# Four moving operands start 32, 16, 96 and 48 bytes past a multiple of 128 in SBUF, where they started 64 bytes past one

## The chip, the cores and the metric

One core of a Trainium2 chip runs the whole program in one launch. The metric is the device time of that launch in microseconds, taken as the median of several runs. The hardware profile is of one more execution.

## What is computed

Two transformer-like blocks over one sequence of 256 tokens with 1024 features, in float32:

```python
for i in range(2):                       # first block
    h = modulate(rmsnorm(x, norm_mix[i]), sh1, sc1)
    y = pool_mixer(h, ...) if i == 0 else moba_attention(h, w_qkv, w_o, rel_bias)
    x = x + g1 * y
    h = modulate(rmsnorm(x, norm_mlp[i]), sh2, sc2)
    a = relu(h @ w_up[i])                # 1024 -> 4096
    x = x + g2 * ((a * a) @ w_down[i])   # 4096 -> 1024
x = rmsnorm(x, norm_final)
z = rmsnorm(x, norm1) @ w_in + b_in      # second block
...                                      # convolution, linear recurrence (gates wa, wx), two output products
m = sigmoid(z_ga) * y_a + sigmoid(z_gb) * y_b
x = x + m @ w_mix_out
h = rmsnorm(x, norm2)
x = x + (silu(h @ ffn_w1) * (h @ ffn_w3)) @ ffn_w2    # 1024 -> 2816 -> 1024
return rmsnorm(x, norm_f)
```

## The kernel before, in words

**Layout.** Activations lie transposed: 128 features of a chunk on the 128 partitions, 256 tokens along the free dimension. A matmul has a 128x128 block of weights as its stationary operand and one chunk of an activation (128 partitions x 256 columns, 1024 bytes in each partition) as its moving operand. The weights come from HBM as a stream of units of eight such blocks, two units to a DMA, into the ring `raw`.

**Three products instead of one.** Most matrix products are made in a reduced float32 format. Each float32 number is split into a high part and the rest: ScalarE writes `w_hi` from `raw` (line 1104), VectorE writes `w_lo = raw - w_hi` (line 1467), and the activations are split in the same way into pairs such as `hid_hi` and `hid_lo`. A product is then high times high, high times low, low times high:

```python
hi = w[0][:, slot, s * P:(s + 1) * P]
pe.matmul(dst, hi, r_hi, ...)      # line 645
pe.matmul(dst, hi, r_lo, ...)      # line 646
...
lo = w[1][:, slot, s * P:(s + 1) * P]
return pe.matmul(dst, lo, r_hi, ...)   # line 651
```

Each of these matmuls has its own weight load (LDWEIGHTS; the profile calls this engine PEld). In a phase made of whole units the eight chunks' high-weight matmuls come first, 16 of them in turns of lines 645 and 646, and then the eight of line 651: 24 to a unit.

**The split activations.** There are six pairs: `pool` (pool mixer), `xg` (the input of the up projections, qkv, glu, rx, rg, conv and ffn), `hid` (the input of the two down projections), `o` (the input of the attention's output projection), `act` (the input of the gates, and later of the mix product) and `f` (the input of the product with ffn_w2, called w2 here). The number of three-product matmuls they take part in follows from the units: 64 units of 24 for `hid` (1536), 8 for `o` (192), 52 blocks of three for the gates (156) and 8 units for mix (192) for `act`, 22 units for `f` (528), and the work of 174 units for `xg` (4176).

**Where they lie.** `LINE` is 128 bytes and `HALF` is 16 float32 (64 bytes). `w_hi` starts at byte 33,920 of each partition and `w_lo` at 50,304, both multiples of 128; so do all their blocks, 512 bytes apart. Ahead of each split activation a filler of `HALF` elements is allocated at a multiple of `LINE`:

```python
def half_line(name, where=ctx):
    where.enter_context(nc.sbuf_tensor(f"{name}_half_line", [P, HALF], F32, align_bytes=LINE))
```

So `hid_hi` starts at 162,496, `hid_lo` at 195,264, `o_hi` at 189,248, `act_hi` at 119,616 and `f_hi` at 109,248: each 64 bytes past a multiple of 128. Chunks of these are 1024 bytes apart, so every chunk is. The chunks of `xg_hi` and `xg_lo` are 288 float32 (1152 bytes, nine times 128) apart, 64 bytes past a multiple of 128 as well; a matmul of the first block reads 258 columns of them (two more carry the modulation's shift), one of the second block 256. The pool mixer's weights have a place of their own: `pool_w_hi` starts at 196,416 and `pool_hi` at 212,800, so there both the weights and the moving operand are 64 bytes past a multiple of 128, and moving operand and weights differ by a multiple of 128.

**Order of the work.** TensorE goes through the phases pool, up0, down0, qkv with the attention between its units, o, up1, down1, glu, rx, rg, gates, gb, ga, lru, conv, mix, ffn, w2. The products with `raw` itself (last two units of rg, gb, ga and lru; lines 977 and 1030) are full float32 and not split. TensorE waits by semaphores for the split weights (`high_ready`, `low_ready`), for the chunks of the moving operand, and for its output bank to be read. No wait, no queue and no order is touched by the change. The functions that read the four operands are `down` (line 824: `hid`), `o_part` (`o`), the gates' loop and `whole("mix", ...)` (`act`), and `halves` with the loop behind it (`f`). They are written by ScalarE (lines 1207, 1258, 1316, 1420) and VectorE (lines 1662, 1786, 1855, 2052, 2054).

Of the kernel before, what the change touches and what calls it, by code (L numbers as in the profile page):

```python
# [12 lines left out]
F32R = mybir.dt.float32r  # L13

P = 128
SEQ = 256
D = 1024
DC = D // P
FFC = 4 * D // P
RC = 1280 // P  # L20
F2C = 2816 // P
# [8 lines left out]
LINE, HALF = 128, 16  # L30
# [184 lines left out]
def build(nc, weights, w_mod, w_dots, c_row, x_in, vectors, rel_bias, buckets, inv_count, identity, out):  # L215
    scratch = nc.dram_tensor("bias_by_distance", [HEADS, 384], F32, kind="Internal").ap()
    with ExitStack() as ctx:
        def sb(name, shape, dt=F32, where=ctx):
            return where.enter_context(nc.sbuf_tensor(name, shape, dt))
# [5 lines left out]
        def half_line(name, where=ctx):  # L225

            where.enter_context(nc.sbuf_tensor(f"{name}_half_line", [P, HALF], F32, align_bytes=LINE))

        raw = sb("raw", [P, RAW, PAIR])  # L230
        w_hi = ctx.enter_context(nc.sbuf_tensor("w_hi", [P, HL, UT * P], F32R, align_bytes=LINE))
        w_lo = sb("w_lo", [P, HL, UT * P], F32R)
# [47 lines left out]
            pool_hi = sb("pool_hi", [P, DC, SEQ], F32R, part)  # L280
            pool_lo = sb("pool_lo", [P, DC, SEQ], F32R, part)
        with ExitStack() as part:
            half_line("hid", part)
            hid_hi = sb("hid_hi", [P, FFC, SEQ], F32R, part)
            hid_lo = sb("hid_lo", [P, FFC, SEQ], F32R, part)
        with ExitStack() as part:
            qT = sb("qT", [P, 2, SEQ], F32, part)
            kT = sb("kT", [P, 2, SEQ], F32, part)
            vT = sb("vT", [P, 2, SEQ], F32, part)
            vtok = sb("vtok", [P, 2, SEQ], F32, part)  # L290
            toep = sb("toep", [P, 2, 2, 384], F32, part)
            logit = sb("logit", [P, 2, 384], F32, part)
            prob = sb("prob", [P, 2, 384], F32, part)
            probn = sb("probn", [P, 2, 384], F32, part)
            pT = sb("pT", [P, 2, 384], F32, part)
            smx = sb("smx", [P, 2, 8], F32, part)
            half_line("o", part)
            o_hi = sb("o_hi", [P, DC, SEQ], F32R, part)
            o_lo = sb("o_lo", [P, DC, SEQ], F32R, part)
        first.close()  # L300
        with ExitStack() as part:
            RXW = SEQ + RTAPS - 1
            UW = SEQ + TAPS - 1
            rx = sb("rx", [P, RC, RXW], F32, part)
            with ExitStack() as inner:
                half_line("act", inner)
                act_hi = sb("act_hi", [P, RC, SEQ], F32R, inner)
                act_lo = sb("act_lo", [P, RC, SEQ], F32R, inner)
            a2 = sb("a2", [P, RC, SEQ], F32, part)
            sb("behind_a2", [P, RC * SEQ + 2 * HALF], F32, part)  # L310
            u = sb("u", [P, DC, UW], F32, part)
            y = sb("y", [P, DC, SEQ], F32, part)
            grg = sb("grg", [P, RC, SEQ], F32, part)
            rt = sb("rt", [P, RC, SEQ], F32, part)
            ig = sb("ig", [P, RC, SEQ], F32, part)
            av = sb("av", [P, RC, SEQ], F32, part)
            sga = sb("sga", [P, DC, SEQ], F32, part)
            sgb = sb("sgb", [P, DC, SEQ], F32, part)
            pool_prod = sb("pool_prod", [P, 2, POOL_TAPS, SEQ], F32, part)
            h32 = sb("h32", [P, DC, SEQ], F32, part)  # L320
        with ExitStack() as part:
            half_line("f", part)
            f_hi = sb("f_hi", [P, F2C, SEQ], F32R, part)
            f_lo = sb("f_lo", [P, F2C, SEQ], F32R, part)
            yout = sb("yout", [P, DC, SEQ], F32, part)

        four = [ctx.enter_context(nc.psum_tensor(f"bank{b}", [P, 512], F32)) for b in range(4)]
# [1891 lines left out]
```

## Time and profile before

| what | value |
|---|---|
| median of 3 runs | 1018.91 us (1015.68 to 1020.47) |
| span of the profiled execution | 1015.1 us, 20313 instructions |
| TensorE matmul, busy | 978.7 us, 96%, 7980 matmuls |
| TensorE weight load, busy | 934.2 us, 92%, 7980 loads |
| VectorE / ScalarE / GpSimd busy | 77% / 55% / 10% |
| mean granted TensorE clock | 0.985 |

The profiled execution is known by its span, from the first to the last instruction; what lies around it is the 3.8 us up to the median. A matmul's own duration in the profile is a latency, from its start to the modelled end of its output, and matmuls overlap. What a stream of them costs is the distance from start to start.

### The profile page before, as it was taken

Reading aid. Unit: us, or ns where it says so; the run is one execution under the profiler, and the core shown is the slowest. Engines: PE = TensorE matmul, PEld = TensorE weight load, DVE = VectorE, ACT = ScalarE, POOL = GpSimd, SP = SyncE. Lnnn points to the kernel's source line nnn. Section 1 sums busy time; section 2 is a strip of 40 time slices with the busy share of each in tenths; the row PEclk is TensorE's granted clock in tenths of the full one; section 3 lists DMA queues with packets and bytes.
Section 4 is the critical chain, followed back from the end, with each engine's and each line's share of the span. In section 5 each row is a group of like instructions: output and inputs, shape, how many; then the busy total and the mean of one; then the engine's idle time right before and its main releaser. Section 6 shows DMA issues by size and latency. Waiting matters only on the chain.

```text
span 1015.1 us, 20313 instructions
## 1 busy us (share of the span) xinstructions
PE 978.7 (96%) x7980; PEld 934.2 (92%) x7980; DVE 780.2 (77%) x1354; ACT 561.6 (55%) x922; POOL 105.3 (10%) x134
## 2 busy tenths in 40 slices
PE   4799999999999999999999999999999999999996
PEld 1479999999999899999999999998889999999996
DVE  4757986888776777677766799999998887777654
ACT  4248676444666658776454566678116564444352
POOL 0000000000000000000000000899920000000000
PEclk9789999999999999999999999999999999999998
DMA  9997797877465855454545555463445555555631
GB/s 376 421 420 315 268 372 301 343 299 284 126 203 156 306 210 206 167 190 169 212 177 184 174 186 192 141 241 128 139 152 207 184 191 196 179 193 179 208 125 42
DMA packets 35883, 222.31 MB, mean 219 GB/s; under 512 B 3883, under 2 KB 9180, under 8 KB 9436
## 3 DMA queue, kind: packets, MB, share of 16 engines
q1 hardware_dynamic: 35804, 221.22, 60.5%
q8 instruction: 55, 0.90, 0.4%
q14 instruction: 24, 0.20, 0.1%
HBM read 220.13 MB, written 1.07 MB: 218 GB/s over the span
## 4 chain that ended last, share of the span: by engine, by line
PE 82%; DVE 9%; ACT 4%; DMA 3%; issue 2%; DVEq 0%; SPq 0%; ACTq 0%
PE bank L645 23%; PE bank L651 22%; PE bank L646 22%; PE bank L977 5%; PE bank L1030 3%; DVE w_lo L1467 2%; PE s_banks L674 2%; DMA mod_raw<-w_mod 1%; ACT w_hi L1104 1%; DVE s_banks L1872 1%; DVE bank L1847 1%; PE s_banks L1030 1%; DMA raw<-weights 1%; DVE ab L1840 1%; DVE mod_raw L1518 1%
## 5 line engine op out<-in xcount | busy, mean ns | idle before, releaser
L1467 DVE TENSOR_TENSOR w_lo<-raw,w_hi 128x1024 fp32r<-128x1024 f32 x284 | 346.2, 1225 | 31.5 <-ACT w_hi L1104 29.1
L1104 ACT ACTIVATE w_hi<-raw 128x1024 fp32r<-128x1024 f32 x284 | 296.8, 1050 | 102.8 <-PE bank L651 99.9
L645 PE MATMUL bank<-xg_hi,w_hi 128*128 128x258 f32 (+1 forms) x1376 | 341.4, 285 | 1.2 <-DVE w_lo L1467 0.8
L646 PE MATMUL bank<-xg_lo,w_hi 128*128 128x258 f32 (+1 forms) x1376 | 337.0, 282 | 0.0
L645 PEld LDWEIGHTS bank<-xg_hi,w_hi 128*128 128x128 f32 x1376 | 260.2, 189 | 6.2 <-issue 5.1
L646 PEld LDWEIGHTS bank<-xg_lo,w_hi 128*128 128x128 f32 x1376 | 260.6, 189 | 0.2
L651 PE MATMUL bank<-xg_hi,w_lo 128*128 128x258 f32 (+1 forms) x1376 | 198.9, 283 | 0.3 <-DVE w_lo L1467 0.3
L651 PEld LDWEIGHTS bank<-xg_hi,w_lo 128*128 128x128 f32 x1376 | 179.0, 189 | 0.8 <-DVE w_lo L1467 0.5
L645 PE MATMUL bank<-hid_hi,w_hi 128*128 128x256 f32 x512 | 123.5, 279 | 0.0
L646 PE MATMUL bank<-hid_lo,w_hi 128*128 128x256 f32 x512 | 123.4, 279 | 0.0
L646 PEld LDWEIGHTS bank<-hid_lo,w_hi 128*128 128x128 f32 x512 | 96.0, 188 | 0.0
L645 PEld LDWEIGHTS bank<-hid_hi,w_hi 128*128 128x128 f32 x512 | 96.0, 188 | 0.0
L1872 DVE SCALAR_TENSOR_TENSOR s_banks<-u,vec,s_banks 128x256 f32<-128x256 f32 x172 | 71.2, 480 | 0.2
L651 PE MATMUL bank<-hid_hi,w_lo 128*128 128x256 f32 x512 | 70.7, 279 | 0.0
L651 PEld LDWEIGHTS bank<-hid_hi,w_lo 128*128 128x128 f32 x512 | 64.8, 188 | 0.0
L977 PE MATMUL bank<-h,raw 128*128 128x256 f32 x288 | 62.5, 379 | 0.0
L977 PEld LDWEIGHTS bank<-h,raw 128*128 128x128 f32 x288 | 54.6, 190 | 7.3
L605 POOL MEMSET rx<- 128x30 f32 x1 | 0.1, 130 | 560.5 <-PE bank L651 560.5
L624 POOL TENSOR_TENSOR y<-y,pool_prod 128x256 f32<-128x256 f32 x60 | 56.6, 963 | 0.1
L614 POOL TENSOR_TENSOR pool_prod<-u,vec 128x256 f32<-128x256 f32 x60 | 48.0, 822 | 76.2 <-PE bank L651 74.0
L1205 ACT ACTIVATE ub<-ab 128x256 f32<-128x256 f32 x64 | 32.6, 509 | 37.6 <-DVE ab L1655 37.5
L1518 DVE CUSTOM_DVE_ANT_0 mod_raw<-mod_raw,c_all,vec 128x1024 f32<-128x1024 f32 x40 | 49.6, 1276 | 0.0
(246 smaller groups left out, 1301.1 us busy)
## 6 DMA issues: line engine op xcount, KB each, us to landing
raw<-weights SPq DMA_DIRECT2D x157, 1024.0 KB, 5.0
mod_raw<-w_mod SPq DMA_DIRECT2D x28, 1024.0 KB, 11.2
mod_raw<-w_dots SPq DMA_DIRECT2D x20, 1024.0 KB, 8.4
toep<-bias_by_distance SPq DMA_DIRECT2D x8, 256.0 KB, 5.5
x<-x_in SPq DMA_DIRECT2D x1, 1024.0 KB, 5.0
toep<-bias_by_distance SPq DMA_DIRECT2D x8, 128.0 KB, 3.9
y_out<-yout SPq DMA_DIRECT2D x4, 256.0 KB, 2.5
c_all<-c_row SPq DMA_DIRECT2D x1, 512.0 KB, 14.7
```

Source lines behind the costliest of these rows:

```text
L614: nc.gpsimd.tensor_tensor(pool_prod[:, k % 2, e, :], u[:, m, k:k + SEQ], col("dw_w", DC * k + m).broadcast_to((P, SEQ)), ALU.mult).then_in ...
L624: nc.gpsimd.tensor_tensor(dst, dst, pool_prod[:, k % 2, e, :], ALU.add).then_inc(pool_tap, 1)
L645: pe.matmul(dst, hi, r_hi, start=start, stop=False, skip_group_check=True)
L646: pe.matmul(dst, hi, r_lo, start=False, stop=False, skip_group_check=True)
L651: return pe.matmul(dst, lo, r_hi, start=False, stop=stop, skip_group_check=True)
L977: mm = pe.matmul(out_bank(name, v)[:, 0:SEQ], raw[:, slot, ((at % 2) * UT + k) * P:((at % 2) * UT + k + 1) * P], src[:, k, 0:SEQ], start=k ...
L1030: mm = pe.matmul(out_bank("lru", m)[:, 0:SEQ], raw[:, slot, ((at % 2) * UT + s) * P:((at % 2) * UT + s + 1) * P], rt[:, k, :], start=k == ...
L1104: act.activation(pool_w_hi[:, at, :] if name == "pool" and at < 2 else w_hi[:, at % HL, :], raw[:, slot, (at % 2) * UT * P:(at % 2 + 1) * ...
L1205: act.activation(ub[:, j % 2, :], ab[:, j % 2, 0:SEQ], ACT.Relu, bias=ab[:, j % 2, SEQ:SEQ + 1]).then_inc(relu_done, 1)
L1467: ve.tensor_tensor(lo, raw[:, slot, (at % 2) * UT * P:(at % 2 + 1) * UT * P], hi.bitcast(F32), ALU.subtract).then_inc(lo_done, 1)
L1518: ve.tensor_tensor_reduce(w, w, c_all[:], 1.0, col("b_mod", at + half), ALU.mult, ALU.add, accum_out=modv[:, at + half:at + half + 1]).the ...
L1872: ve.scalar_tensor_tensor(dst, u[:, m, k:k + SEQ], col("dw_w", DC * k + m), src, ALU.mult, ALU.add)\
```

## The change

After the change the four pairs `hid`, `o`, `act` and `f` are each one tensor that starts at a multiple of 128 bytes and of which the first `at` float32 are left unused. `at` is 8, 4, 24 and 12, that is 32, 16, 96 and 48 bytes. High and low halves are views of it. The pairs `xg` and `pool` and the weights stay where they are, and the instructions and their order are the same.

```diff
+        def past_line(name, count, at, where):
+            whole = where.enter_context(nc.sbuf_tensor(name, [P, count * SEQ + at], F32R, align_bytes=LINE))
+            return whole[:, at:at + count * SEQ].rearrange("p (c n) -> p c n", n=SEQ)
...
-            half_line("hid", part)
-            hid_hi = sb("hid_hi", [P, FFC, SEQ], F32R, part)
-            hid_lo = sb("hid_lo", [P, FFC, SEQ], F32R, part)
+            hid = past_line("hid", 2 * FFC, 8, part)
+            hid_hi, hid_lo = hid[:, 0:FFC, :], hid[:, FFC:2 * FFC, :]
...
-            half_line("o", part)
-            o_hi = sb("o_hi", [P, DC, SEQ], F32R, part)
-            o_lo = sb("o_lo", [P, DC, SEQ], F32R, part)
+            o = past_line("o", 2 * DC, 4, part)
+            o_hi, o_lo = o[:, 0:DC, :], o[:, DC:2 * DC, :]
...
-                half_line("act", inner)
-                act_hi = sb("act_hi", [P, RC, SEQ], F32R, inner)
-                act_lo = sb("act_lo", [P, RC, SEQ], F32R, inner)
+                act_both = past_line("act_both", 2 * RC, 24, inner)
+                act_hi, act_lo = act_both[:, 0:RC, :], act_both[:, RC:2 * RC, :]
...
-            half_line("f", part)
-            f_hi = sb("f_hi", [P, F2C, SEQ], F32R, part)
-            f_lo = sb("f_lo", [P, F2C, SEQ], F32R, part)
+            f_both = past_line("f_both", 2 * F2C, 12, part)
+            f_hi, f_lo = f_both[:, 0:F2C, :], f_both[:, F2C:2 * F2C, :]
```

The tensors now start at 162,432 (`hid`), 189,184 (`o`), 119,552 (`act_both`) and 109,184 (`f_both`), and the operands that many bytes plus 32, 16, 96 and 48.

## Rows read from the trace of the kernel before

**Rows 1.** The page: busy time, and the granted clock in 40 slices.

```profile
PE 978.7 (96%) x7980; PEld 934.2 (92%) x7980; DVE 780.2 (77%) x1354; ACT 561.6 (55%) x922; POOL 105.3 (10%) x134
...
PEclk9789999999999999999999999999999999999998
```

**Rows 2.** The page: the chain that ended last, by engine.

```profile
PE 82%; DVE 9%; ACT 4%; DMA 3%; issue 2%; DVEq 0%; SPq 0%; ACTq 0%
```

**Rows 3.** Chain of waits, 168 to 264 us, down0: start us, duration us, piece.

```profile
191.85 0.94 PE bank L651 x8
...
205.98 0.94 PE bank L651 x8
208.81 0.94 PE bank L651 x8
...
217.29 0.94 PE bank L651 x8
```

**Rows 4.** Chain of waits, 944 to 1006 us, w2.

```profile
949.69 0.91 PE bank L651 x8
952.41 0.91 PE bank L651 x8
...
966.01 0.91 PE bank L651 x8
```

**Rows 5.** Chain of waits, 797 to 822 us, mix.

```profile
806.01 0.91 PE bank L651 x8
808.74 0.91 PE bank L651 x8
...
819.62 0.91 PE bank L651 x8
```

**Rows 6.** Timeline, 363 to 380 us, o: start us, duration us, engine, line, instruction.

```profile
364.14 0.28 PE L645 MATMUL bank<-o_hi,w_hi 128*128 128x256 f32 x1
...
365.32 0.28 PE L646 MATMUL bank<-o_lo,w_hi 128*128 128x256 f32 x1
...
368.93 0.28 PE L646 MATMUL bank<-o_lo,w_hi 128*128 128x256 f32 x1
...
370.41 0.28 PE L651 MATMUL bank<-o_hi,w_lo 128*128 128x256 f32 x1
```

**Rows 7.** Timeline, 60 to 62 us, pool mixer.

```profile
60.59 0.28 PE L645 MATMUL bank<-pool_hi,pool_w_hi 128*128 128x256 f32 x1
...
61.55 0.28 PE L651 MATMUL bank<-pool_hi,pool_w_lo 128*128 128x256 f32 x1
```

**Rows 8.** Chain of waits, up1 (384 to 472 us), then ffn (850 to 940 us).

```profile
404.68 0.96 PE bank L651 x8
...
439.40 0.96 PE bank L651 x8
```

```profile
865.14 0.94 PE bank L651 x8
...
904.62 0.94 PE bank L651 x8
```

**Rows 9.** Instructions by tile hid_hi, then f_hi: count, duration ns min/median/max, starts.

```profile
L645 PE MATMUL bank<-hid_hi,w_hi x512: 279/279/286, 170.0 to 561.3; 128*128 128x256 f32 x171
L1207 ACT ACTIVATE hid_hi<-ub x64: 417/419/422, 82.2 to 473.3; 128x256 fp32r<-128x256 f32 x48, 128x256 f32 x16
```

```profile
L645 PE MATMUL bank<-f_hi,w_hi x132: 276/276/361, 944.9 to 1003.7; 128*128 128x256 f32 x132
```

**Rows 10.** Timeline, 370.4 to 371.2 us, o, weight loads with matmuls.

```profile
370.52 0.19 PEld L646 LDWEIGHTS bank<-o_lo,w_hi 128*128 128x128 f32 x1
...
370.63 0.28 PE L646 MATMUL bank<-o_lo,w_hi 128*128 128x256 f32 x1
370.64 0.19 PEld L651 LDWEIGHTS bank<-o_hi,w_lo 128*128 128x128 f32 x1
```

**Rows 11.** Timeline, 199.9 to 200.2 us, down0, weight load with its matmul.

```profile
199.93 0.19 PEld L646 LDWEIGHTS bank<-hid_lo,w_hi 128*128 128x128 f32 x1
...
200.05 0.28 PE L646 MATMUL bank<-hid_lo,w_hi 128*128 128x256 f32 x1
```

## The prediction

> **What bounds the kernel now.** The page's busy line and clock line come first: TensorE's matmuls are busy 96% of the span, its weight loads 92%, and the granted clock is at full speed, 2.4 GHz, in all but the first and last slices [rows 1]. The chain that ended last lies on TensorE for 82% of the span [rows 2], and in the stages of this change it runs from matmul to matmul with hardly anything between. So the kernel is as long as its matmuls are apart, and the reader should look at one number, the distance from the start of one matmul to the start of the next. Nothing is removed or added by this change, no wait and no instruction; only where four moving operands begin. It can act only through that distance, and the question is whether the distance depends on the address.
>
> **The distance as it is.** In the chain each unit of 24 matmuls shows once, at its eight matmuls of line 651. In down0 two neighbours start 2.83 us apart, 118 ns to a matmul; over nine units it is 25.44 us / 216 = 117.8 ns [rows 3]. Down1 goes at the same pace. In w2 a unit takes 2.72 us, and six take 16.32 us: 113.3 ns [rows 4]. Mix has 13.61 us for five units: 113.4 ns [rows 5]. The o projection shows both: ten matmuls in 1.18 us, 118 ns, and some 4 us later thirteen in 1.48 us, 114 ns [rows 6]. All these operands lie 64 bytes past a multiple of 128 and their weights on one. So at one alignment there are two steady paces, 117.8 and 113.3 ns, and a stage can stay in the slow one for 1536 matmuls. The durations agree: a matmul with `hid_hi` takes 279 ns, one with `f_hi` 276 [rows 9]. In the fast pace a weight load starts 0.11 us ahead of its matmul and the next load 0.01 us behind that matmul's start [rows 10]; in the slow pace it is 0.12 us [rows 11]. That chain, load, matmul, next load, makes the 113 ns, which is more than the 107 ns that 256 columns take at 2.4 GHz (256 / 2.4). I read 113.3 as the floor of this stream and what lies above it as the two reads getting in each other's way.
>
> **What other addresses cost.** Two stages show it. In the pool mixer, moving operand and weights differ by a multiple of 128 bytes, not by 64 more; at full clock eight matmuls take 0.96 us, 120.0 ns each [rows 7]. And the `xg` operand, whose chunks lie 1152 bytes apart and so change their place against the weights' blocks in every larger power of two, goes at 39.48 us / 336 = 117.5 ns with 256 columns and 34.72 us / 288 = 120.6 ns with 258 [rows 8]. So for 256 columns the trace holds the paces 113.3, 117.5 to 117.8 and 120.0, the last where the difference is 0 modulo 128. None lies at 16, 32, 48 or 96 bytes; their cost has to be bounded between these.
>
> **The change part by part.** Now the terms are: `hid`, 1536 matmuls at 117.8; `o`, 192 at a mixture of the two paces, of which I take 114.5; `act`, 156 in the gates and 192 in mix, 348 together, at 114.2 by the same kind of mixture in the gates; `f`, 528 at 113.4.
>
> I interpolate in a straight line by the distance from 64: 113.3 ns at 64 bytes, 120.0 at 0 (or 128), which is 6.7 ns for 64 bytes, 1.67 ns for each 16. Then:
> - `hid` at 32 bytes, 32 off: 116.7 ns, 1.1 less than now. 1536 x 1.1 = 1.7 us gained.
> - `o` at 16 bytes, 48 off: 118.3, 3.8 more. 192 x 3.8 = 0.7 us lost.
> - `act` at 96 bytes, 32 off: 116.7, 2.5 more. 348 x 2.5 = 0.9 us lost.
> - `f` at 48 bytes, 16 off: 115.0, 1.6 more. 528 x 1.6 = 0.8 us lost.
>
> The sum is +0.7 us, 1018.9 + 0.7 = 1019.6. The profiled execution's span would go from 1015.1 to 1015.8, the 3.8 us around it staying.
>
> The bounds from the same rows. Below: nothing in the trace goes under 113.3, so `hid` can gain at most 4.45 ns, 1536 x 4.45 = 6.8 us, and `o` and `act` 1.2 and 0.9 ns, 0.5 us together: -7.4. Above: all four at the pool mixer's 120.0 is 2.2 x 1536 = 3.4, 5.5 x 192 = 1.1, 5.8 x 348 = 2.0 and 6.6 x 528 = 3.5 us: +10.0. I take the line since the four places lie between the two that are measured, and keep both ends.
>
> The writers of these operands cost nothing: ScalarE's write of `hid_hi` takes 419 ns [rows 9], ScalarE and VectorE are busy 55 and 77% [rows 1], and TensorE hides them. Even 50 ns more on each would meet TensorE only where the first matmul of o waits for its operand. If TensorE got 4% faster in down, the weight splitting (one unit of it per 2.7 us against 1.2 us of VectorE's and 1.0 of ScalarE's time) would still be ahead. Phases whose operands do not move, `xg` above all, have a pattern that repeats from unit to unit, so how they are entered should not matter.
>
> The Trainium skill speaks against all of this. "TensorE: Matmul & The Clock Gate", under the phases of a matmul, says that TensorE reads SBUF through two independent ports and that loading the next weights doesn't steal bandwidth from the running matmul; by that the distance doesn't depend on the two addresses and the sum is 0. The paces in the rows, 113.3 against 120.0, don't agree with it fully, though they don't show that the address is the cause either.
>
> **The rivals.**
> - *The address does nothing.* The paces are then two ways in which the stream falls into step by how a stage is entered, as the o projection shows with both at one alignment [rows 6], and pool's 120.0 comes from its few matmuls behind a halt. Each stage keeps about its pace: 0 us, 1018.9. The port rule of the Trainium skill in the paragraph above is this rival's. Against it: eight times exactly 120.0, a pace seen with 256 columns in no other stage.
> - *`hid` comes loose from the slow pace.* If 32 bytes has no stable slow pace, or one close to 113.3, the down projections gain their 6.8 us, with the others anywhere between -0.5 and +1: 1011.5 to 1013. For it: o and mix leave the slow pace by themselves, and only `hid` stays. Against it: 64 was the one place of which the trace shows the fast pace at all.
 It costs 5.1 us as soon as the four average 118.1 ns (the average now is 2604 matmuls at 116.2, and 5.1 / 2604 is 2.0 ns more), and 10.0 us at 120.0: 1024 to 1028.9. For it: 258 columns, which reach just past a 64-byte piece, cost 3 ns more where two columns at 2.4 GHz are 0.8 [rows 8], and all four new places cross such pieces.
>
> The page "SBUF — State Buffer" of the Trainium skill, under the SBUF cachelines, gives lines of 16 bytes. All four places are multiples of 16, so by that no matmul would touch a line more than now, and this rival's argument from 64-byte pieces falls; no row here shows lines of either size by itself.
>
> **How the numbers follow.** A change within 0.5%, 5.1 us, is about what a measurement of this kernel can't tell from none. The interpolated case, with its own range of 1015.5 to 1023.5 (some stages fast, some slow), gets 0.32; no effect 0.12; `hid` loose 0.24; the collision 0.32. So faster 0.24, same 0.44, slower 0.32. The range takes in both bounds, 1018.9 - 7.4 and 1018.9 + 10.0, trimmed little since both ends are plain cases of their own: 1011.5 to 1028.
>
> **What would show each step.** Right: a unit of the down projections takes about 2.80 us in the chain where it took 2.83, one of w2 2.76 for 2.72, one of mix 2.80, and ffn and up1 stay at 2.82 and 2.89. Wrong: 2.72 in the down projections is the second rival, 2.83 and 2.72 unchanged everywhere is the first, 2.88 in all is the third. A pace below 2.72 us a unit in any stage would show that the floor I took is none. A stage that changes between two paces within itself would say that entering decides more than the address. A change in ffn or up1 of more than 0.02 us a unit would mean that something else than the four operands' places is at work.

## The result, and the profile after

| | before | after |
|---|---|---|
| median of 18 runs each | 1018.06 us | 1019.60 us |
| all runs | 1014.60 to 1020.47 | 1018.28 to 1021.33 |
| ratio | | 1.0019, 95% interval 1.0011 to 1.0028 |
| profiled execution | span 1015.1 us | 1020.19 us, span 1018.4 us |

The change costs 0.19%: a small loss, clear of the noise of these runs, and within the 0.5% that were called no change. The predicted time, 1019.6 us, was the measured one, but that it fits so well is luck. The sum started from 1018.9, where 18 runs of the kernel before give 1018.06, and added 0.7 us where the medians differ by 1.5. And the terms of the sum don't fit the paces in the trace, which add up to more than what was measured.

The page of the kernel after, busy time, clock and the chain by engine (beside [rows 1] and [rows 2]):

```profile
PE 980.6 (96%) x7980; PEld 936.5 (92%) x7980; DVE 779.9 (77%) x1354; ACT 561.2 (55%) x922; POOL 105.2 (10%) x134
...
PEclk9799999999999999999999999999999999999998
...
PE 82%; DVE 9%; ACT 4%; DMA 3%; issue 2%; DVEq 0%; SPq 0%; ACTq 0%
```

Nothing moved between engines, so the distance between matmuls is again the number to read. From here on it is called the pace. It is taken from the chain as before: start of the eight matmuls of the low-weight line (653 now) in one unit, against a later unit, over 24 matmuls a unit.

The chain of the kernel after in down0, down1, mix and w2 (against [rows 3], [rows 5] and [rows 4]):

```profile
207.64 0.94 PE bank L653 x8
...
258.52 0.94 PE bank L653 x8
...
474.01 0.93 PE bank L653 x8
...
496.41 0.93 PE bank L653 x8
...
806.13 0.95 PE bank L653 x8
...
820.33 0.95 PE bank L653 x8
...
950.61 0.95 PE bank L653 x8
...
967.65 0.95 PE bank L653 x8
```

Down0: 50.88 us for 18 units, 117.8 ns. Down1: 22.40 us for 8 units, 116.7. Mix: 14.20 us for 5, 118.3. W2: 17.04 us for 6, 118.3. The o projection, from its timeline (against [rows 6]):

```profile
369.95 0.28 PE L653 MATMUL bank<-o,w_lo 128*128 128x256 f32 x1
...
371.97 0.28 PE L648 MATMUL bank<-o,w_hi 128*128 128x256 f32 x1
```

17 matmuls in 2.02 us, 118.8 ns. Up1 and ffn, which read `xg`, stand where they stood [rows 8]: 404.63 to 430.67 us is nine units, 120.6 ns; 868.72 to 908.20 is fourteen, 117.5.

```profile
404.63 0.96 PE bank L653 x8
...
430.67 0.96 PE bank L653 x8
...
868.72 0.94 PE bank L653 x8
...
908.20 0.94 PE bank L653 x8
```

So in the traces the change costs 528 x 4.9 = 2.6 us in w2, 348 x 4.1 = 1.4 in the gates and mix, 192 x 4.2 = 0.8 in o, and gives 768 x 1.1 = 0.85 in down1: +4.0 us. The two spans differ by 3.3 only, since the execution before happened to reach down0 1.2 us later: its first matmul with `hid` starts at 170.0 us [rows 9], that of the execution after at 168.8.

```profile
L647 PE MATMUL bank<-hid,w_hi x512: 277/278/282, 168.8 to 560.4; 128*128 128x256 f32 x171
```

### The profile page after: what moved, and what is told of

It is laid out like the page before. It is cut to its first block, busy times and chain, and to the rows that moved or that the text cites. A ratio compares the mean times of both kernels' runs of the same rounds, so it can differ in the third digit from the quotient of the medians.

```text
span 1018.4 us, 20329 instructions
## 1 busy us (share of the span) xinstructions
PE 980.6 (96%) x7980; PEld 936.5 (92%) x7980; DVE 779.9 (77%) x1354; ACT 561.2 (55%) x922; POOL 105.2 (10%) x134
## 4 chain that ended last, share of the span: by engine, by line
PE 82%; DVE 9%; ACT 4%; DMA 3%; issue 2%; DVEq 0%; SPq 0%; ACTq 0%
PE bank L647 23%; PE bank L653 22%; PE bank L648 22%; PE bank L979 5%; PE bank L1032 3%; DVE w_lo L1469 2%; DMA mod_raw<-w_mod 1%; PE s_banks L676 1%; ACT w_hi L1106 1%; DVE s_banks L1874 1%; DVE bank L1849 1%; PE s_banks L1032 1%; DMA raw<-weights 1%; DVE ab L1842 1%; DVE mod_raw L1520 1%
## 5 line engine op out<-in xcount | busy, mean ns | idle before, releaser
L648 PE MATMUL bank<-hid,w_hi 128*128 128x256 f32 x512 | 123.0, 280 | 0.0
L647 PE MATMUL bank<-hid,w_hi 128*128 128x256 f32 x512 | 122.9, 279 | 0.0
L648 PEld LDWEIGHTS bank<-hid,w_hi 128*128 128x128 f32 x512 | 96.5, 188 | 0.0
L647 PEld LDWEIGHTS bank<-hid,w_hi 128*128 128x128 f32 x512 | 96.0, 187 | 0.0
L653 PE MATMUL bank<-hid,w_lo 128*128 128x256 f32 x512 | 70.4, 279 | 0.0
L653 PEld LDWEIGHTS bank<-hid,w_lo 128*128 128x128 f32 x512 | 64.6, 188 | 0.0
```

The source lines that it names most:

```text
L647: pe.matmul(dst, hi, r_hi, start=start, stop=False, skip_group_check=True)
L648: pe.matmul(dst, hi, r_lo, start=False, stop=False, skip_group_check=True)
L653: return pe.matmul(dst, lo, r_hi, start=False, stop=stop, skip_group_check=True)
```

## The experiments

Every ratio below is to the kernel before, timed in the same set of runs. Two theories were set against each other. **Place**: the pace depends on the moving operand's address less the weights', modulo some power of two. **Entry**: the stream of load, matmul, next load has several steady paces, and how it enters a stage picks one. Below, a *place* is that difference modulo 256 bytes. Before, `hid` and `f` are at place 64 and `o` and `act` at 192 (their tensors start at another multiple of 128). The change's 32, 16, 96 and 48 are the places 32, 144, 224 and 48. The code cuts of e2, e3 and e4 are against e1, that of e12 against e8, that of e11 against the kernel before, and the others against the kernel after. Each run has one profile, so every pace below is that of one execution.

**e1, every operand back at its address of before (`hid` and `f` at place 64, `o` and `act` at 192), in the new form.**

```diff
-            hid = past_line("hid", 2 * FFC, 8, part)
+            hid = past_line("hid", 2 * FFC, 16, part)
...
-            o = past_line("o", 2 * DC, 4, part)
+            o = past_line("o", 2 * DC, 16, part)
```

and 16 for `act_both` and `f_both`.

> All four operands at 64 bytes again, in the changed kernel's form (one tensor with unused elements ahead), so every address is that of the kernel before. Address theory: a ratio of 1.000, hid at 117.8 ns from matmul to matmul, w2 and mix at 113.3. The rival that the pace is a matter of how a stage is entered: the paces may differ from those in the profile of before even though no address does (a down projection at 113.3, or w2 at 117.8), since it is another execution.

Ratio 0.9992 (0.9979 to 1.0006). Hid 117.8 in both down projections, mix and w2 113.3, as in the first profile. But o's last stretch (95 matmuls) is at 117.8 in this execution where it was at 113.3, at the same address. From its timeline in e1:

```profile
368.93 0.28 PE L647 MATMUL bank<-o,w_hi 128*128 128x256 f32 x1
...
371.05 0.28 PE L647 MATMUL bank<-o,w_hi 128*128 128x256 f32 x1
```

18 matmuls in 2.12 us, 117.8 ns, where [rows 6] have thirteen in 1.48 us. So the form costs nothing, and one place holds two paces.

**e2, the change's `hid` alone; e5, the change's other three alone.**

```diff
-            hid = past_line("hid", 2 * FFC, 16, part)
+            hid = past_line("hid", 2 * FFC, 8, part)
```

> hid at 32 bytes as changed, the other three at 64. Address theory: down1 at 116.67 and down0 at 116.67 or 117.8 ns as in the profile after, w2 and mix at 113.3, gates and o at 113.3 to 114.5; 0.9 to 1.7 us faster than before (ratio 0.998 to 0.999). If only entering matters: o, act and f may be slow here too, and the ratio is 1.00 to 1.004.

> hid stays at 64 bytes, o, act and f at 16, 96 and 48 as changed: the other part of the change alone. If the places cost what the profile after shows (118.7, 118.3 and 118.3 ns for 114.5, 114.2 and 113.4): 0.8 + 1.4 + 2.6 = 4.8 us slower than before, ratio 1.0047, down projections at 117.8. If the change's small total hides a gain elsewhere: less than 1.003.

e2: ratio 0.9998 (0.9984 to 1.0011); down0 117.8, down1 116.7 again, mix and w2 113.3. The 0.85 us of down1 lies inside the interval. e5 has 4, 24 and 12 elements for `o`, `act_both` and `f_both` and 16 for `hid`: ratio 1.0058 (1.0042 to 1.0073), about 5.9 us, for 4.8 expected; both down projections at 117.8, mix and w2 at 118.3. W2 in the chain of e5, 14.20 us for 5 units:

```profile
950.23 0.95 PE bank L653 x8
...
964.43 0.95 PE bank L653 x8
```

So the loss is in the three small operands, and `hid`'s move is nearly neutral. The paces at the moved places are the same to 0.1 ns in the kernel after and in e2 or e5, so there they belong to place and stage.

**e3, all four at a multiple of 128.** 0 for all four.

```diff
-            hid = past_line("hid", 2 * FFC, 16, part)
+            hid = past_line("hid", 2 * FFC, 0, part)
```

> All four at a multiple of 128 bytes, no difference from the weights modulo 128. Address theory (collision as in the pool mixer): 120.0 ns in all four, 3.4 + 1.1 + 2.0 + 3.5 = 10 us slower than before, ratio 1.010. Rival that the address does nothing: paces of 113.3 and 117.8 and a ratio of 1.000 to 1.004.

Ratio 1.0071 (1.0052 to 1.0090), 1023.93 us. The chain of e3 in down0 and w2:

```profile
169.85 0.96 PE bank L653 x8
...
192.89 0.96 PE bank L653 x8
...
950.82 0.96 PE bank L653 x8
...
973.86 0.96 PE bank L653 x8
```

Each pair is 23.04 us for 8 units, 120.0 ns: `hid` and `f` (place 0) have the pool mixer's pace [rows 7]. O and mix (place 128) are at 118.5 to 118.7. That the address does nothing is excluded. Place 0 and place 128 differ too, though in different stages here.

**e4, `hid` 128 bytes further.** It stays 64 past a multiple of 128 and goes from place 64 to place 192.

```diff
-            hid = past_line("hid", 2 * FFC, 16, part)
+            hid = past_line("hid", 2 * FFC, 48, part)
```

> hid 128 bytes further than before: still 64 past a multiple of 128, but its difference from the weights is now 192 modulo 256 where it was 64. o and act have 192 and fall into the fast pace by themselves; hid and f have 64, hid stayed slow and f turned fast behind a halt. If the period that matters is 256 bytes, both down projections go at 113.3 ns, 6.8 us faster than before (ratio 0.993). If the period is 128 bytes, nothing changes: 117.8 ns, ratio 1.000.

Ratio 0.9935 (0.9917 to 0.9954), 1010.60 us: 6.6 us gained. The chain of e4 in down0 and down1:

```profile
204.99 0.91 PE bank L653 x8
...
226.75 0.91 PE bank L653 x8
...
469.06 0.91 PE bank L653 x8
...
490.82 0.91 PE bank L653 x8
```

21.76 us for 8 units in both, 113.3 ns where [rows 3] have 117.8. The instructions by tile agree: 276 ns for a matmul with `hid` where it was 279 [rows 9].

```profile
L647 PE MATMUL bank<-hid,w_hi x512: 276/276/286, 167.7 to 553.0; 128*128 128x256 f32 x171
```

**e6 and e7, a scan of places**, timed once each.

```diff
-            hid = past_line("hid", 2 * FFC, 8, part)
+            hid = past_line("hid", 2 * FFC, 40, part)
...
-            f_both = past_line("f_both", 2 * F2C, 12, part)
+            f_both = past_line("f_both", 2 * F2C, 52, part)
```

with 56 and 12 for `o` and `act_both`; in e7 it is 32, 24, 28 and 20 for `hid`, `f_both`, `o` and `act_both`.

> A scan of places, given as the moving operand's address less the weights' modulo 256: hid at 160, f at 208, act at 176, o at 224. If only 192 is good and each 16 bytes away cost as steps towards 120: f and act 115 to 117 ns, hid 116 to 118, o 116 to 118.7. If the fast pace is a range around 192, f at 208 and act at 176 are at 113.3.

> The scan's second half: hid at 128, f at 96, act at 208, o at 112 (addresses modulo 256 less the weights'). o and act had 118.5 to 118.7 at 128 in the run with all four at multiples of 128, so hid should have 118.6 here if the pace is a matter of the address difference alone, and not of the stage. f at 96: between 117.8 (64) and 118.6 (128). o at 112: the same. act at 208 tells whether 16 bytes past 192 is still fast.

1022.79 and 1023.45 us, slower than all but e3. The two texts misstate `o`'s place: its tensor starts at a multiple of 256, so 56 and 28 elements put it at 96 and 240, not at 224 and 112. Of all places tried, steady paces in ns:

| place | paces seen, with the stage |
|---|---|
| 0 | 120.0 down0, down1, w2 |
| 32 | 117.8 down0, 116.7 down1 (twice each) |
| 48 | 118.3 w2 (twice) |
| 64 | 117.8 down0 and down1 in four programs; 113.3 and 117.8 w2; 117.8 o and mix (e11) |
| 96 | 120.0 w2 and o |
| 128 | 120.0 down0, 118.7 down1, 118.5 to 118.7 mix and o |
| 144 | 118.7 o |
| 160 | 118.7 down0, 117.3 down1 |
| 176 | 119.2 mix |
| 192 | 113.3 and 117.8 in o, gates, mix, ffn and w2; down0 and down1 113.3 in four programs, 117.8 in e11 |
| 208 | 119.2 w2, 116.7 mix, both in the gates |
| 224 | 118.3 mix and gates |
| 240 | 117.2 o |

W2 at 208 and mix at 208, from the chains of e6 and e7:

```profile
949.97 0.95 PE bank L653 x8
...
975.71 0.95 PE bank L653 x8
```

```profile
808.75 0.93 PE bank L653 x8
...
819.95 0.93 PE bank L653 x8
```

25.74 us for 9 units, 119.2 ns, and 11.20 us for 4, 116.7: already 16 bytes away from 192 the fast pace is gone. It was seen at 64 and 192 and nowhere else, and two stages at one place can differ by 2.5 ns. With `hid` at 128, down1 has 118.7 where it had 120.0 at place 0 (e3), so the two are not one place.

**e9, a push at the entry.** The addresses of e1, and a matmul of four columns into an unused corner of a bank ahead of each down projection.

```diff
             def first_down(name):
 
+                pe.matmul(stat_bank[:, 300:304], ones[:], pick[:], start=True, stop=True)
```

> All operands at 64 as before, and one small matmul (4 columns, into an unused corner of a bank) ahead of each down projection. It only disturbs the step in which the stream enters the stage. If the pace at 64 is a matter of entry (as f, that turned fast behind a halt): one or both down projections at 113.3 ns instead of 117.8, 3.4 or 6.8 us faster, ratio 0.9935 to 0.9967. If 64 modulo 256 has only the slow pace for hid: both at 117.8 and ratio 1.000.

Ratio 1.0021 (1.0009 to 1.0033). Neither down projection left 117.8. But w2, whose addresses are those of the kernel before, went to it, in the chain of e9:

```profile
952.02 0.94 PE bank L653 x8
...
974.63 0.94 PE bank L653 x8
```

22.61 us for 8 units, 117.8 ns where [rows 4] have 113.3. That is 528 x 4.4 = 2.3 us, about what the ratio says. The push missed its aim; it shows that at place 64 w2 has both paces.

**e11, the weights moved in place of `hid`.** The kernel before, `w_hi` and `w_lo` 128 bytes further and everything else 256.

```diff
+        ctx.enter_context(nc.sbuf_tensor("ahead_w_hi", [P, 2 * HALF], F32, align_bytes=LINE))
         w_hi = ctx.enter_context(nc.sbuf_tensor("w_hi", [P, HL, UT * P], F32R, align_bytes=LINE))
         w_lo = sb("w_lo", [P, HL, UT * P], F32R)
+        sb("behind_w_lo", [P, 2 * HALF])
...
-            bkt = sb("bkt", [33, 384], F32, part)
+            bkt = ub[0:33, :, :].rearrange("p a n -> p (a n)")[:, 0:384]
```

> The kernel before, its operands at the same places modulo 256, but the split weights 128 bytes further modulo 256 (w_hi and w_lo at a multiple of 256, where they were 128 past one). hid is then at 192 from the weights without having moved. If the difference of the two addresses sets the pace: both down projections at 113.3 ns, 6.8 us faster, ratio 0.9935, as with hid moved. If the moving operand's own address does: both at 117.8, ratio 1.000. o, act and f go from 192 and 64 to 64 and 192 and may take either of the two paces.

Ratio 1.0007 (0.9995 to 1.0019): no gain. `hid` is at 192 from its weights, with the very difference of addresses that it has in e4, and still slow. Chain and instructions by tile of e11:

```profile
171.82 0.94 PE bank L653 x8
...
205.74 0.94 PE bank L653 x8
```

```profile
L647 PE MATMUL bank<-hid_hi,w_hi x512: 281/281/282, 169.8 to 561.5; 128*128 128x256 f32 x171
```

33.92 us for 12 units, 117.8 ns. The duration is 281 ns, not the 279 of place 64 [rows 9]. All slow stages fit this: 279 at place 64 (`hid` before, w2 in e9), 281 at 192. So the difference of the addresses does mark how the two reads meet, but place 192 doesn't by itself give the fast pace. My reading of e4, that it does, fell here. The rival that was named ahead of this run, the moving operand's own address, came out as it said. `hid` is slow in the five profiled programs in which it starts 192 bytes past a multiple of 256 (the kernel before, e1, e5, e9, e11), and fast in the four in which it starts 64 past one (e4, e8, e10, e12). As a rule for every stage it fails: `f`, 192 past one, ran at 113.3 in the kernel before and at 117.8 in e9, and mix, 64 past one, at 113.3 in the kernel before and at 117.8 in e11. For `hid` no run excludes it.

**e8, e10 and e12, more operands at 192.** In e8 `hid` and `f` are at 192, and the second block reads and writes `xg` through views with chunks 1024 bytes apart, so that these 2064 matmuls are at 192 throughout; with 1152 between chunks they are at 64 and 192 in turn.

```diff
+        def by_1024(t, at):
+            return t[:].rearrange("p c n -> p (c n)")[:, at:at + DC * SEQ].rearrange("p (c n) -> p c n", n=SEQ)
+
+        xs_hi, xs_lo = by_1024(xg_hi, 0), by_1024(xg_lo, 2 * HALF)
...
-                    whole("glu", v // 8, v % 8, xg_hi, xg_lo, SEQ)
+                    whole("glu", v // 8, v % 8, xs_hi, xs_lo, SEQ)
```

> hid and f at 192 modulo 256 from the weights, o and act there already, and the xg operand of the second block (glu, rx, rg, conv, ffn: 2064 matmuls) with its chunks 1024 bytes apart at 192, where they were 1152 apart and so at 64 and 192 in turn. Address theory with a period of 256 bytes: these go from 117.5 to 113.3 ns, 8.6 us, of which up to 1.8 us (rx and rg, where the chain runs over VectorE) may be lost, beside the 6.8 us of hid: 1002 to 1004 us, ratio 0.985 to 0.987. If xg's 117.5 has another cause than the alternation, ratio 0.993 as with hid alone.

Ratio 0.9902 (0.9883 to 0.9920), 1005.48 us; less than hoped. The chain of e8 in ffn, and in mix:

```profile
821.65 0.91 PE bank L658 x8
...
843.41 0.91 PE bank L658 x8
```

```profile
795.98 0.94 PE bank L658 x8
...
810.12 0.94 PE bank L658 x8
```

Ffn went to 113.3 ns (21.76 us for 8 units) from 117.5 [rows 8]. Conv and mix hung at 117.8 (14.14 us for 5 units in mix), though at 192 like the rest. From glu to the end of rg TensorE's matmuls ran at 113.4 but took 94.7 us for 96.6, not the 3.4 us less that 816 matmuls should give. It waits for VectorE's `w_lo` three times in the program, 1.2 us in all, of which two times and 0.9 us lie in this stretch; there the kernel before has no such wait:

```profile
PE bank L658 <- DVE w_lo L1474: 1.2, 3, 0.6
```

(the waits of e8: who waited for whom, us in total, times, longest us).

e10 puts the first block's `xg` at 192 as well, with chunks 1280 bytes apart.

```diff
-ROW = 288
+ROW = 320
...
+            xg = part.enter_context(nc.sbuf_tensor("xg", [P, 48 + 2 * DC * ROW], F32R, align_bytes=LINE))
...
+        xs = ctx.enter_context(nc.sbuf_tensor("xs", [P, 48 + DC * SEQ], F32R, align_bytes=LINE))
```

> Every split operand but the pool mixer's with all its chunks at 192 modulo 256 from the weights; the first block's xg has its chunks 1280 bytes apart instead of 1152. Address theory: the 258-column matmuls of up0, qkv and up1 (2112) go from 120.5 to between 113.3 and 114.2 ns, 13 to 15 us less, beside what the second block's xg (8.6 us, less where conv and mix hang in the slow pace) and hid (6.8) give: 987 to 991 us, ratio 0.970 to 0.975. If 258 columns cost their 3 ns whatever the place (they reach past a 64-byte piece): 116 ns, 9 us less, ratio 0.980. If xg's stride alone is no cause there: ratio 0.990 as without this.

Ratio 0.9919 (0.9896 to 0.9942). A plain miss. Up1 in the chain of e10:

```profile
384.89 0.97 PE bank L655 x8
...
408.09 0.97 PE bank L655 x8
```

23.20 us for 8 units, 120.8 ns with 258 columns, where 1152-byte chunks have 120.6 [rows 8]. So for 258 columns, having every chunk at 192 gained nothing. And w2, conv, mix and ffn all hung at 117.8 in this execution. Its six runs lie between 1006.85 and 1013.55 us.

e12 is e8 with conv back on 1152-byte chunks.

```diff
-            first_two("conv", xs_hi, xs_lo, SEQ, (ln_lo, 0))
+            first_two("conv", xg_hi, xg_lo, SEQ, (ln_lo, 0))
```

> As e8 (hid, f and the second block's xg at 192), but conv reads xg with chunks 1152 bytes apart as before. If a slow pace is handed on from stage to stage (conv and mix hung at 117.8 in e8, while mix behind a conv with 1152 was at 113.3 in all runs at 64 past a multiple of 128): conv 117.5, mix 113.3, 0.85 us less than e8, ratio 0.989. If mix's pace is set by its own place: mix as in e8, 117.8, ratio 0.990.

Mix and w2 in the chain of e12:

```profile
795.80 0.91 PE bank L658 x8
...
809.40 0.91 PE bank L658 x8
...
938.06 0.94 PE bank L658 x8
...
960.67 0.94 PE bank L658 x8
```

Mix is at 113.3 ns (13.60 us for 5 units) with its own place untouched: only what runs ahead of it changed. In the other five profiles with mix at place 192 behind a conv with 1152 bytes between chunks (the kernel before, e1, e2, e4, e9) it is at 113.3 as well, and in the two behind a conv at 192 (e8, e10) at 117.8. That speaks for entry, though one such execution can't show it: w2, whose own place and whose ffn ahead of it are those of e8, stood at 117.8 here (22.61 us for 8) and at 113.3 in e8. The ratio is 0.9888 (0.9874 to 0.9902), 1005.36 us, the fastest of all; its interval overlaps that of e8.

**What the theories are worth now.** Neither is enough alone. The place bounds which paces were seen: 64 and 192 have 113.3 and 117.8, all others tried have one or two between 116.7 and 120.0. Something besides the place picks among them, and at 64 and 192 the pick mostly holds for a whole stage (o changed within itself behind a stop, [rows 6]). That it is the entry is the likeliest reading, and not shown. Open is the rule of that pick. `hid` took the slow pace at 64 in four profiled programs (the kernel before, e1, e5, e9), the fast one at 192 in four with the weights in place (e4, e8, e10, e12), and the slow one at 192 when the weights were moved (e11), which moves `xg`, the operand ahead of it, against them too. How the preceding stage's places hand over was not tried by itself; e10 moved them too, beside much else, and `hid` stayed fast.

## Why the prediction was right, and which terms were not

- *What bounds the kernel, and that only the pace can change*: right. Busy shares, clock and chain are the same, and `xg`'s stages kept 120.6 and 117.5.
- *120.0 ns as the price of place 0, read from the pool mixer*: right. E3 has it in 1536 + 528 matmuls.
- *"I interpolate in a straight line by the distance from 64"*: this step failed. The pace doesn't fall with the distance from 64. W2 was to be at 115.0, 16 bytes off, and is at 118.3, more than three times the term (+2.6 us for +0.8). `act` was to be at 116.7 and is at 118.3 (+1.4 us for +0.9). `o` was to be at 118.3 and is at 118.7 to 118.8 (+0.8 for +0.7). `hid` was to be at 116.7 and is so in down1 but not in down0 (-0.85 us for -1.7). The sum by the traces is +4.0 us, not +0.7. Of the signs that were named for this case (2.80 us a unit in the down projections, 2.76 in w2, 2.80 in mix) only down1's came; down0 stood at 2.83, and w2 and mix went to 2.84.
- *Why the total fits all the same*: in part by luck. The base was 0.85 us too high and the change 0.8 us too small, and the two cancel. The 3.8 us kept around the span are not around it: time less span is about 1.8 us in every profiled execution whose time is on record, so the profiled execution before took about 1017, a us under its median. The measured loss is 1.5 us between medians, 1.1 to 2.9 by the interval, less than the 4.0 of the traces. Two things on record are large enough for that. The kernel before was timed in five sets of runs, and its medians are 1018.06, 1017.40, 1015.45, 1017.54 and 1017.00 us; the kernel after was timed in the first alone, where the kernel before was slowest. And executions differ by themselves: in the fourteen profiles the first matmul with `hid` starts anywhere between 167.6 and 170.0 us, and o and w2 had either pace at one address (w2's is worth 2.3 us). Which of these made up the difference is not shown, since the unprofiled runs leave no trace. E5, in the set with 1015.45, measured 5.9 us where the traces give 4.8, so the difference can have either sign.
- *The floor of 113.3 ns*: held in all fourteen profiles; no steady three-product pace lies below it. That the chain load, matmul, next load of [rows 10] makes it was not tested.
- *"The address does nothing"* (0.12, with the port rule of the Trainium skill, "TensorE: Matmul & The Clock Gate", phases of a matmul): excluded by e3, 120.0 ns in the down projections and w2 against 113.3 for the same instructions in e4. Its other half, that something besides the address decides the pace, was right (e9, e11).
- *"`hid` comes loose"* (0.24): not at 32, but when it was moved to 192, with the 6.8 us that were worked out (6.6 measured in e4); not when the weights were moved instead (e11).
- *"Whatever isn't 64 off collides"* (0.32): right that no place but 64 and 192 has the fast pace, at 116.7 to 120.0 ns; wrong that all go to 118 to 120 (down1 at place 32 has 116.7, faster than before) and that 64 off is enough (`hid` was slow there). The reason given, a line of 128 bytes or pieces of 64, isn't shown.
- The 3 ns of two columns more were no evidence on places: with every chunk at 192, 256 columns went from 117.5 to 113.3 ns (e8) and 258 stayed at 120.8 (e10).
- The 16-byte lines of the Trainium skill ("SBUF — State Buffer", SBUF cachelines) don't tell the places apart: all are multiples of 16 and their paces run from 113.3 to 120.0.

## What to carry to other kernels

When a kernel is a dense stream of weight load and matmul, read the distance between starts stage by stage before anything else: 4.4 ns more in each of 1536 matmuls is 6.8 us that no busy share shows. Try the moving operand's start, with all its chunks, 64 and 192 bytes past the weights modulo 256, by moving the operand itself (moving the weights gave nothing, e11), and judge by the stage's pace in several executions, since one place can have two paces. Don't interpolate between two measured addresses.

## What was not expected of the hardware

- The same instructions with the same addresses ran a whole stage at 113.3 or at 117.8 ns: w2 in the kernel before and in e9 (which adds two small matmuls far ahead of it). The last 95 matmuls of o did the same in the kernel before and in e1.
- Sixteen bytes beside 192, w2 ran at 119.2 ns and mix at 116.7, where 192 gives 113.3.
- A slow stage has a matmul duration of 279 ns at place 64 and 281 at place 192, at one and the same pace of 117.8.
- With 258 columns the pace was 120.6 and 120.8 ns for two chunk strides (1152 and 1280 bytes), where 256 columns had 117.5 with 1152 bytes between chunks and 113.3 with 1024.
- Two programs with one and the same difference between the addresses of `hid` and its weights ran it at 113.3 (e4) and at 117.8 ns (e11).
